# A block sweep with one row tile of the array per head and one masked copy per level and recurrence

## The reference

```
def chunked_gated_recurrence(q, k, v, log_decay):
    # S_t = diag(exp(log_decay_t)) S_{t-1} + k_t v_t^T ; o_t = S_t^T q_t (per head, causal)
    ...
    b = jnp.cumsum(gc, axis=3)
    rel = b[:, :, :, :, None, :] - b[:, :, :, None, :, :]
    pair_decay = jnp.exp(jnp.minimum(rel, 0.0)) * causal[:, :, None]
    scores = jnp.einsum('bhnid,bhnjd,bhnijd->bhnij', qc, kc, pair_decay)
    o_intra = jnp.einsum('bhnij,bhnjv->bhniv', scores, vc)
    ...
for l in range(DEPTH):
    n = rms_norm(h, norm_mix[l])
    ...
    h = h + jnp.concatenate([y_a, y_b, y_c], axis=-1) @ w_mix_out[l]
    h = h + memory_cross_attention(...)
    h = h + conv_glu_ffn(...)
```

## Time and profile before

| | us |
|---|---|
| median of 3 runs | 1569.75 |
| lowest and highest | 1569.43, 1570.15 |
| profiled execution, span of its instructions | 1568.1 |
| block sweep, layer 1 (220.73 to 250.30) | 29.57 |
| block sweep, layer 2 (995.10 to 1024.66) | 29.56 |

### The profile page before, as it was taken

How to read it: one execution, slowest core, us unless ns; L and a number is a source line. 1 busy time by engine, 2 the same in 40 slices (tenths; PEclk the granted TensorE clock), 3 DMA queues, 4 the chain that set the end, 5 groups by cost and what they waited for, 6 DMA issues and landing times. The chain is left out here.

```text
span 1568.1 us, 18614 instructions
## 1 busy us (share of the span) xinstructions
PE 1477.2 (94%) x6967; PEld 1196.0 (76%) x6967; DVE 783.0 (50%) x1505; ACT 596.9 (38%) x1053; POOL 638.7 (41%) x338
## 2 busy tenths in 40 slices
PE   6997889999999999999989898889999999999997
PEld 5886657787788888888868775678867888888886
DVE  4289468335376504653133965772345663055620
ACT  5524554457433212232154146633564322122220
POOL 5433621453343444444335254423523444444342
PEclk9998999999999999999999899999999999999999
DMA  5322001332233233333143220012322332333321
GB/s 146 96 80 68 27 1 41 94 108 68 81 94 94 88 101 95 94 94 100 35 118 95 68 81 1 1 65 84 118 68 70 95 106 88 90 106 89 99 87 74
DMA packets 172975, 125.81 MB, mean 80 GB/s; under 512 B 11825, under 2 KB 149840, under 8 KB 172880
## 3 DMA queue, kind: packets, MB, share of 16 engines
q1 hardware_dynamic: 172880, 124.56, 26.7%
HBM read 122.44 MB, written 2.10 MB: 79 GB/s over the span
## 5 line engine op out<-in xcount | busy, mean ns | idle before, releaser
L552 POOL TENSOR_TENSOR w_lo<-raw,w_hi 128x1024 fp32r<-128x1024 f32 (+2 forms) x230 | 544.5, 2371 | 789.2 <-ACT w_hi L938 789.1
L938 ACT ACTIVATE w_hi<-raw 128x1024 fp32r<-128x1024 f32 (+2 forms) x230 | 236.7, 1033 | 354.6 <-PE bank L599 349.0
L597 PE MATMUL bank<-x_hi,w_hi 128*128 128x512 f32 (+1 forms) x880 | 349.7, 397 | 0.3 <-DVE x_lo L1221 0.3
L598 PE MATMUL bank<-x_lo,w_hi 128*128 128x512 f32 (+1 forms) x880 | 347.8, 395 | 0.0
L599 PE MATMUL bank<-x_hi,w_lo 128*128 128x512 f32 (+1 forms) x880 | 347.8, 395 | 0.0
L597 PEld LDWEIGHTS bank<-x_hi,w_hi 128*128 128x128 f32 (+1 forms) x880 | 164.7, 187 | 41.7 <-issue 1.0
L598 PEld LDWEIGHTS bank<-x_lo,w_hi 128*128 128x128 f32 (+1 forms) x880 | 164.7, 187 | 41.0 <-issue 1.0
L599 PEld LDWEIGHTS bank<-x_hi,w_lo 128*128 128x128 f32 (+1 forms) x880 | 164.7, 187 | 40.7
L597 PE MATMUL bank<-w_hi,x_hi 128*128 128x512 f32 (+1 forms) x448 | 168.7, 376 | 18.7 <-POOL w_lo L552 12.5
L1289 DVE TENSOR_TENSOR h<-h,bank 128x512 f32<-128x512 f32 x64 | 44.0, 688 | 250.3 <-PE bank L599 250.2
L599 PE MATMUL bank<-w_hi,x_lo 128*128 128x512 f32 (+1 forms) x448 | 165.2, 369 | 0.0
(11 more groups left out here) (266 smaller groups left out, 1930.6 us busy)
## 6 DMA issues: line engine op xcount, KB each, us to landing
raw<-in_w_ffn_in SPq DMA_DIRECT2D x88, 512.0 KB, 3.8
raw<-in_w_ffn_out SPq DMA_DIRECT2D x40, 512.0 KB, 3.7
raw<-in_w_in SPq DMA_DIRECT2D x36, 512.0 KB, 3.7
raw<-in_w_mix_out SPq DMA_DIRECT2D x16, 512.0 KB, 3.8
raw<-in_w_ca_kv SPq DMA_DIRECT2D x32, 256.0 KB, 3.3
raw<-in_w_ca_q SPq DMA_DIRECT2D x8, 512.0 KB, 3.9
raw<-in_w_ca_out SPq DMA_DIRECT2D x8, 512.0 KB, 3.8
h<-in_x SPq DMA_DIRECT2D x4, 512.0 KB, 5.0
```

The costliest lines, as they stand in the source:

```text
L552: pool.tensor_tensor(w_lo[i % SPLIT][:, 0:n], raw[i % RAW][:, 0:n], w_hi[i % SPLIT][:, 0:n].bitcast(f32), ALU.subtract).then_inc(S["lo_spl ...
L597: pe.matmul(o, ah, bh, start=first, stop=False)
L598: pe.matmul(o, ah, bl, start=False, stop=False)
L938: act_.activation(w_hi[k % SPLIT][:, 0:n], raw[k % RAW][:, 0:n], ACT.Copy).then_inc(S["hi_split"], 1)
```

## The change

- `Qx`, `expand`, its clearing on POOL and the semaphore `qx_done` go. PE multiplies K by Q itself, one matmul for each head and tile of the sequence: K's rows of that head (32 partitions for GLA, 64 for HGRN2) against Q's rows of that head, 64 query columns. These are row tiles of the array: four for GLA, two for HGRN2. A level has 32 matmuls of 64 query columns, 16 for GLA and 16 for HGRN2; before it had 12 (at m = 32, 24). The slices at m >= 32 go too.
- Each row tile writes its own bank: GLA head r writes bank r, all four tiles of the sequence side by side (256 columns); HGRN2 heads use banks 4 and 5 at one level and 6 and 7 at the next (`HGRN_BANKS`). All banks are now slices of one PSUM tensor.
- `sweep_mm` and `swept` count one for each level and recurrence. A PE group waits for `q_level` (Q scaled) and `k_level` (K scaled) of its recurrence and for its banks.
- DVE takes all of a recurrence's scores with one masked copy of 128x1024 over four or two banks. The scores are laid out head by head, and `pair_mask` is four times as wide. DVE scales Q only after this level's matmuls, since they now read Q.
- POOL writes the diagonal in twelve operations instead of eight, for the new layout (elements as before).
- The wide `pair_mask` is made once, ahead of the layers, by one copy of 128x1792 instead of 128x448.

```diff
-        pair_mask = sb("pair_mask", [P, len(LEVELS), P // 2], u8)
+        pair_mask = sb("pair_mask", [P, len(LEVELS), NT * P // 2], u8)
...
-        scores_g = place("scores_g", 8, [P, NT, NH, P])
-        scores_h = place("scores_h", 24, [P, NT, NH, P])
+        scores_g = place("scores_g", 8, [P, NH, NT, P])
+        scores_h = place("scores_h", 24, [P, NH, NT, P])
...
-        pb = [ctx.enter_context(nc.psum_tensor(f"bank{i}", [P, 512], f32)) for i in range(8)]
+        psum = ctx.enter_context(nc.psum_tensor("psum", [P, 8 * 512], f32))
+        pb = [psum[:, 512 * i:512 * (i + 1)] for i in range(8)]
...
-                dve.tensor_copy(pair_mask[:, :, :], pairs[:, :, :])
+                dve.tensor_copy(pair_mask[:, :, :].rearrange("p l (n q) -> p l n q", n=NT),
+                                pairs[:, :, :].unsqueeze(2).to_broadcast([P, len(LEVELS), NT, P // 2]))
...
+        HGRN_BANKS = (4, 6)
...
-                pool.wait_ge(S["qkT_mm"], 4 * NT)
-                for x in range(2):
-                    pool.memset(Qx[x][0][:, :, :], 0.0).then_inc(S["zeroed"], 1)
-
...
                 pool.wait_ge(S["pv_mm"], NH)
-                for x in range(2):
-                    pool.memset(Qx[x][1][:, :, :], 0.0).then_inc(S["zeroed"], 1)
                 pool.memset(state[:, :, :], 0.0).then_inc(S["zeroed"], 1)
                 for li, m in enumerate(LEVELS):
                     for x, f in enumerate((slice(0, 1), slice(1, 3))):
-                        pool.wait_ge(S["sweep_mm"], 2 * NT * li + NT * (x + 1))
+                        pool.wait_ge(S["sweep_mm"], 2 * li + x + 1)
...
                 for li, m in enumerate(LEVELS):
                     for x in range(2):
-                        pe.wait_ge(S["qx_done"], 2 * li + x + 1)
+                        pe.wait_ge(S["q_level"], 2 * li + x + 1)
                         if li:
                             pe.wait_ge(S["k_level"], 2 * (li - 1) + x + 1)
+                        if x == 0:
+                            for b in range(NH):
+                                claim(b)
+                        else:
+                            for r in range(2):
+                                claim(HGRN_BANKS[li % 2] + r)
                         for n in range(NT):
-                            b = NT * x + n
-                            claim(b)
-                            bank = pb[b][:, 0:NH * P // 2].rearrange("p (h c m) -> p h c m", h=NH, m=m)
-                            q = Qx[x][li % 2][:, :, n * P:(n + 1) * P].rearrange("p h (c two m) -> p h c two m", two=2, m=m)
...
+                            for f in range(1 + x):
+                                for r in range(2 if x else NH):
+                                    dk = HDK if x else GDK
+                                    rows_ = slice(dk * r, dk * (r + 1))
+                                    bank, c = (HGRN_BANKS[li % 2] + r, 256 * f) if x else (r, 0)
+                                    q = Q[rows_, x + f, n * P:(n + 1) * P].rearrange("p (c two m) -> p c two m", two=2, m=m)
+                                    mm = pe.matmul(pb[bank][:, c + 64 * n:c + 64 * (n + 1)].rearrange("p (c m) -> p c m", m=m),
+                                                   K[rows_, x + f, n * P:(n + 1) * P], q[:, :, 1, :], start=True, stop=True)
+                        mark(mm, S["sweep_mm"])
...
-                def expand(li, x, hd):
-
-                    f, r0, dk = (0, GDK * hd, GDK) if x == 0 else (1 + hd // 2, HDK * (hd % 2), HDK)
-                    r = slice(r0, r0 + dk)
-                    dst, src = (odd_blocks(a, LEVELS[li]) for a in (Qx[x][li % 2][r, hd:hd + 1, :], Q[r, f:f + 1, :]))
-                    ex = act_.activation(dst, src, ACT.Copy)
-                    if hd == NH - 1:
-                        ex.then_inc(S["qx_done"], 1)
-
...
-                    for x in range(2):
-                        dve.wait_ge(S["qx_done"], 2 * li + x + 1)
+                    mask = pair_mask[:, li, :].rearrange("p (b m) -> p b m", m=m).unsqueeze(1).to_broadcast([P, NH, SEQ // (2 * m), m])
+                    for x, sc in enumerate((scores_g, scores_h)):
+                        dve.wait_ge(S["sweep_mm"], 2 * li + x + 1)
                         next_queries(x, m)
-                    mask = pair_mask[:, li, :].rearrange("p (c m) -> p c m", m=m).unsqueeze(1).to_broadcast([P, NH, P // (2 * m), m])
-                    for x, sc in enumerate((scores_g, scores_h)):
-                        for n in range(NT):
-                            dve.wait_ge(S["sweep_mm"], 2 * NT * li + NT * x + n + 1)
-                            bank = pb[x * NT + n][:, 0:NH * P // 2].rearrange("p (h c m) -> p h c m", h=NH, m=m)
-                            dve.copy_predicated(odd_blocks(sc[:, n], m), mask, bank).then_inc(S["swept"], 1)
+                        if x:
+                            b0 = 512 * HGRN_BANKS[li % 2]
+                            found = psum[:, b0:b0 + 1024].rearrange("p (h b m) -> p h b m", h=NH, m=m)
+                        else:
+                            found = psum[:, 0:2048].rearrange("p (h q) -> p h q", h=NH)[:, :, 0:256].rearrange("p h (b m) -> p h b m", m=m)
+                        if li:
+                            dve.wait_ge(S["swept"], 2 * (li - 1) + x + 1)
+                        dve.copy_predicated(odd_blocks(sc[:, :, :, :].rearrange("p h n q -> p h (n q)"), m), mask, found
+                                            ).then_inc(S["swept"], 1)
```

More of the change, by code:

```diff
@@ L234, in build_trunk @@
         q_tok, k_tok = place("q_tok", R3, [P, NT, NH * QK]), place("k_tok", R3 + 12, [P, NT, NH * QK])
-        Qx = [[place(f"Qx{x}_{i}", kb + 8 * x, [P, NH, SEQ]) for i, kb in enumerate((R3 + 4, R0))] for x in range(2)]
         qk = place("qk", R0, [P, 3, SEQ])
@@ L515, in recurrences @@
             def recurrences(pool):
-                pool.wait_ge(S["qkT_mm"], 4 * NT)
-                for x in range(2):
-                    pool.memset(Qx[x][0][:, :, :], 0.0).then_inc(S["zeroed"], 1)
                 pool.wait_ge(S["diag_evac"], 1)
-                for x, sc in enumerate((scores_g, scores_h)):
-                    for n in range(NT):
-                        c = DIAG + 8 * n + NH * x
-                        pool.tensor_tensor(sc[:, n], ident[:, :].unsqueeze(1).to_broadcast([P, NH, P]),
-                                           small[:, c:c + NH].unsqueeze(2).to_broadcast([P, NH, P]), ALU.mult
+                for n in range(NT):
+                    c = DIAG + 8 * n
+                    eye = ident[:, :].unsqueeze(1)
+                    pool.tensor_tensor(scores_g[:, :, n, :], eye.to_broadcast([P, NH, P]),
+                                       small[:, c:c + NH].unsqueeze(2).to_broadcast([P, NH, P]), ALU.mult
+                                       ).then_inc(S["scores_base"], 1)
+                    by_row = small[:, c + NH:c + 2 * NH].rearrange("p (f r) -> p r f", f=2)
+                    for r in range(2):
+                        pool.tensor_tensor(scores_h[:, 2 * r:2 * r + 2, n, :], eye.to_broadcast([P, 2, P]),
+                                           by_row[:, r, :].unsqueeze(2).to_broadcast([P, 2, P]), ALU.mult
                                            ).then_inc(S["scores_base"], 1)
@@ L777, in _ @@
                     for x in range(2):
-                        pe.wait_ge(S["qx_done"], 2 * li + x + 1)
+                        pe.wait_ge(S["q_level"], 2 * li + x + 1)
                         if li:
                             pe.wait_ge(S["k_level"], 2 * (li - 1) + x + 1)
-                        for n in range(NT):
-                            b = NT * x + n
-                            claim(b)
-                            bank = pb[b][:, 0:NH * P // 2].rearrange("p (h c m) -> p h c m", h=NH, m=m)
-                            q = Qx[x][li % 2][:, :, n * P:(n + 1) * P].rearrange("p h (c two m) -> p h c two m", two=2, m=m)
-                            parts = [(2 * m * c, m, slice(c, c + 1)) for c in range(P // (2 * m))] if m >= 32 else \
-                                [(0, P, slice(0, P // (2 * m)))]
-                            for j, nj, cs in parts:
-                                for f in range(1 + x):
-                                    hs = slice(0, NH) if x == 0 else slice(2 * f, 2 * f + 2)
-                                    mm = pe.matmul(bank[j:j + nj, hs, cs, :], K[:, x + f, n * P + j:n * P + j + nj],
-                                                   q[:, hs, cs, 1, :], start=True, stop=True)
-                            mark(mm, S["sweep_mm"])
-                            freed[b] = (S["swept"], 2 * NT * li + b + 1)
@@ L797, in _ @@
+                        mark(mm, S["sweep_mm"])
+                        if x:
+                            for r in range(2):
+                                freed[HGRN_BANKS[li % 2] + r] = (S["swept"], 2 * li + 2)
+                        else:
+                            for b in range(NH):
```

(4 more changed lines are left out.)

34 lines of the change are left out of this document (9 added, 25 removed).

## The result

The changed kernel takes 1573.96 us (median of 15 runs, 1572.45 to 1575.79) against 1569.98 for the kernel before on the same chip: a ratio of 1.0026, 95% interval 1.0018 to 1.0033. The forecast was 5.5 us faster; it is 4 us slower.

What follows compares the result with a forecast made beforehand. PE bounds the kernel (94% busy), but in the changed sweep DVE leads a tie with PE and ACT. Two layers at -2.83 us plus 0.2 at the start give -5.5, so 1564.3 us, range 1559.5 to 1591.

Steps and rivals of the forecast that it cites:

- What bounds the stage; DVE, PE and ACT tied: Sweep stretches, 29.57 us a layer: three engines tied from m = 4 to 16, DVE ahead, so a gain must shorten DVE.
- Row tiles side by side: PE in the sweep: row tiles load at the same time, GLA's group 0.87 us, HGRN2's 1.76, a level 2.65.
- Rival 2: PE in the sweep: row-tile loads go one by one, 3.6 us a group, 7.2 a level, 1614 us; chance 0.17.
- rival 1: PE in the sweep: GLA group of 1.79 us at full clock, 1570.9 us, no change; chance 0.13.
- Merged copies: DVE in the sweep: one 1024-element copy takes 1.14 us, 2.09 at m = 1 and 2; saves 1.95 and 1.13 a layer.
- rival 4: DVE's merged copies cost what four cost, 1568.8 us, or lose the slow rate, 1559; inside the forecast's range.
- The first wait: First level of the sweep: DVE must wait for all 16 GLA matmuls before scaling Q, +1.29 us a layer.
- Scaling of Q taken over at its old price, POOL's products "hidden": Sweep levels: DVE's two scalings take 0.93 us together; POOL's key products, 1.9 us a level, hide under 3.2.
- The clock: PE's granted clock in the sweep: 1.00 in the forecast, with levels of 3.2 us and a stage of 26.7.
- Rival 3: Sweep: the clock stays low, loads take twice as long, 9.7 us more a layer, 1589.3 us; chance 0.08.
- ACT's copies, POOL's clearings: Sweep and attention: ACT loses 56 copies a layer of 0.42 us, POOL four clearings; both gain 0.
- The start: Ahead of the layers: the wide mask's copy grows from 0.39 to at most 1.9 us, +0.2, between 0 and 0.35.

Runs made afterwards that it cites:

- e1: The kernel before with small reserved scratch and a gap, so every tile lies where the changed kernel has it, no instruction changed: 1549.19 us.
- e4: The kernel before with merged masked copies alone, one of 1024 elements a level and recurrence instead of four of 256: 1569.28 us.
- e3: The changed kernel plus filler, full 128 x 128 f32 matmuls on PE whose results nobody reads: 1554.78 us.
- e10: The changed kernel with the filler of e3, same number and columns, but on 32 rows of the array instead of 128: 1587.95 us.
- e2: The changed kernel with a 192-byte gap behind the wide mask, putting the work area back at its old place modulo 512: 1592.4 us.
- e9: The kernel before with its own scratch and only a 320-byte gap between the masks and the work area: 1548.25 us.
- e6: e3 with one more wait: POOL's product on K starts only after DVE has scaled Q of the same recurrence: median 1566.87 us.

## Why the prediction was wrong, step by step

Against e1, which has after's addresses, the loss is 25.6 us, split here by the starts of the same matmuls in the two traces. 0.4 stands before the first layer's gate matmul, 11.6 between it and the first transpose of the memory tokens in layer 1, 11.5 there in layer 2, and 2.1 between, 1.7 of which is one more stretch at half clock that e1 doesn't have:

```profile
834.00:837.40 3.40, 3.40 (x13) 3.40 (x12) 0.00 (x0) 1.11 (x2) 2.47 (x2) 0.51 0.91 255
```

The 21.3 us of the addresses (spans 1568.1 and 1546.8) go off, which leaves the measured 4.3.

- **What bounds the stage; DVE, PE and ACT tied**: right for before. e4 shows it from the other side: shorter DVE alone gives nothing.
- **Row tiles side by side**: right, 0.88 and 1.80 us for 0.87 and 1.76. Rival 2 is out: by it each group would have taken 3.6 us at full clock. The 0.13 that the chances give to rival 1 stood for a GLA group of 1.79 us at full clock and a time of 1570.9, no change. No run shows such a group: its 32 records pass in 0.88 us.
- **Merged copies**: right at m = 4 and above (1.13 for 1.14), mis-sized at m = 1 and 2 (2.27 for 2.09). The step took the fixed part of 0.06 us over to the slow rate; there four copies cost as much as one (2.26 and 2.27), so nothing fixed is saved. That is 4 x 0.18 = 0.7 us a layer, inside the bounds given. (The lower bound does not come out of its own terms: 1.14 at all levels would be -6.6 us a layer, not the -5.6 of rival 4. e4 rules that end out anyway.)
- **The first wait**: the +1.29 of the sum is a DVE idle for 996.39 - 995.18 = 1.21 us from the end of `x_lo`; measured are 1.49. I had PE start 0.05 us behind the end of `x_lo`, as in the trace of before; it is 0.20 (997.10 to 997.30). The rest is the group, 1.28 us from its start to DVE's for 1.16.
- **Scaling of Q taken over at its old price, POOL's products "hidden"**: wrong at full clock. The 0.93 us of a level came from a pair of scalings that had begun before POOL's product; the change lets POOL's product and DVE's scaling go off on the same signal. The six levels m = 1 to 32 take 27.2 us in e3 and 23.1 in the forecast, and DVE is never idle in them. From start to start the twelve scalings take 9.04 us for 5.58, so 3.5 of the 4.2 us are theirs and 0.7 the copies'. The trace of before could have warned: one pair there began behind POOL's products and took 1018.59 - 1017.25 = 1.34 us for 0.93:

```profile
1017.25 1.42 DVE L1390 TENSOR_TENSOR Q<-Q,decay_x 128x256 f32<-128x256 f32 x2
1018.59 1.42 DVE L1413 COPY_PREDICATED scores_g<-pair_mask,bank 128x256 f32<-128x256 uint8 x4
```
```profile
1016.13 1.66 POOL L544 TENSOR_TENSOR K<-K,decay_x 128x512 f32<-128x512 f32 x2 [0.96 <-PE bank L792]
```

  In the changed kernel itself this costs little, because at half clock PE is the bound from m = 4 on.
- **The clock**: this is the step that failed. The sum has every level at clock 1.00; in the change it is 0.50 from the first level on, a level takes PE 5.5 us instead of 2.65, and the stage 40.5 instead of 26.7. Rival 3 had the right mechanism, and nearly the right price: 9.7 us a layer over the kernel before, measured 10.9. It had a chance of 0.08. I argued from the share of time that PE is busy in levels 1 and 2, and took a busy PE for a held clock. e10 shows that PE can be busy all the time and lose it.
- **The tail**: the clock stays down behind the sweep too. The last matmul on the scores is another 3.4 to 3.5 us late, of which about 2.6 are made good before the memory's transposes; another 0.3 a layer is gained ahead of the sweep. The prediction had no term for any of this.
- **The edit that I costed by its copy alone**: the wide mask, +0.2 us in the sum. Its width moves the work area to where the weights stand modulo 512, and that is worth -21 us, more than any term in the sum (e1, e2, e9). So it is luck that the result, 1573.96 us, lies in the middle of the range of 1559.5 to 1591: rival 3's 1589.3 us is e2's kernel (1592.4), and without the addresses the result would have stood at the upper end of the range or over it.
- **ACT's copies, POOL's clearings**: worth nothing, as said. **The start**: +0.4 for +0.2.

## What to carry to other kernels

Small f32 matmuls ran side by side as row tiles (32 records of 32 rows in 0.88 us, four of them in 0.11), but each record still brought a load of 128 columns, and with little of the array at work the clock fell even where PE never paused (e10: 0.50, busy 8.91 of 8.91 us). Look at the granted clock first. In this kernel it stayed at 1.00 in the sweep with the full tiles and their padded zeros, and at 0.50 with the row tiles that replaced them.

An edit that widens a tile moves all behind it, even where it issues nothing. Before the sum is made, compare where the operands of the most frequent matmul lie; here 320 spare bytes beat every edit of the code (e9, 1548.25 us for 1568.38). And if two engines are released by one signal, look for a row in which they started together before pricing either.

## What was not expected of the hardware

- f32r matmuls of 512 columns at full clock start 227 ns apart where work area and weights lie 0 or 256 bytes apart modulo 512, and 229 or 233 ns, by operand, where they lie 64 or 192 apart; 233 at 384.
- The first four row tiles of 32 rows start within 20 ns of each other, the later fours within 50, and each four 0.11 us behind the last; the 32 records of GLA's 16 f32 matmuls pass in 0.88 us.
- The clock stays at 0.50 for 47.7 and 44.3 us, in levels of which PE runs row tiles without a gap (5.53 of 5.53 us).
- DVE's scaling of Q (128x512, both operands in SBUF) takes 1.49 us from start to start where it begins 0.07 us behind POOL's product (e3), and 0.59 ahead of it (e6); a masked copy of 128x1024 from PSUM takes 1.23 to 1.25 either way.
- The same kernel, e6, runs anywhere from 1553.7 to 1574.5 us, as its mean clock goes from 0.982 to 0.964.
